# Weight sums of seven-product groups made in device memory instead of on VectorE, and more such groups: eight in each of three down stages, six in each of two

## What is computed

```python
# first block: ffn_w1 is 2048 x 8192, ffn_w2 is 8192 x 2048
hn = rms_norm(h, norm_ffn[i])
h = h + jnp.square(jax.nn.relu(hn @ ffn_w1[i])) @ ffn_w2[i]
...
# second block: w_down is 5632 x 2048
return (jax.nn.silu(gate) * val) @ w_down
```

## Time and profile before

| | us |
|---|---|
| median of 3 runs | 2193.94 (2193.53 to 2194.72) |
| profiled execution | 2195.73 |
| its span, first to last instruction | 2193.9 |
| PE busy | 2180.1 (99%) |
| DVE, ACT, POOL busy | 1566.5, 1133.5, 711.8 |
| the DMA queue that loads weights, share of 16 engines | 55.7% |

### The profile page before, as it was taken

One profiled execution on the slowest core, in us unless ns is written; L12 is line 12 of the kernel. 1 busy time (PEld: TensorE's weight loads), 2 busy tenths in 40 slices (PEclk: granted clock), 3 DMA queues, 4 the chain that ended last, 5 costly groups with the idle time before them and its releaser, 6 DMA issues.

```text
span 2193.9 us, 34076 instructions
## 1 busy us (share of the span) xinstructions
PE 2180.1 (99%) x11511; PEld 1862.4 (85%) x11511; DVE 1566.5 (71%) x2187; ACT 1133.5 (52%) x1720; POOL 711.8 (32%) x625
## 2 busy tenths in 40 slices
PE   9999999999999999999999999999999999999998
PEld 7888988888888888888888887788888888888887
DVE  6876767558657757755878667567778777787775
ACT  6445555545445545454556455465455455554553
POOL 3202320361362263153000033005554355533531
PEclk9999999999999999999999999999999999999999
DMA  7665335556556556566565654545555665555664
GB/s 250 231 224 171 116 130 181 174 184 211 191 182 209 192 184 207 202 194 197 177 199 188 225 171 137 192 163 182 189 195 185 202 198 192 188 191 197 200 207 149
DMA packets 118084, 414.35 MB, mean 189 GB/s; under 512 B 12896, under 2 KB 18048, under 8 KB 117472
## 3 DMA queue, kind: packets, MB, share of 16 engines
q1 hardware_dynamic: 111600, 401.37, 55.7%
q10 hardware_dynamic: 6384, 11.70, 1.7%
HBM read 409.29 MB, written 2.15 MB: 188 GB/s over the span
## 4 chain that ended last, share of the span: by engine, by line
PE 93%; DVE 4%; ACT 1%; DMA 1%; POOL 1%; issue 1%; SPq 0%; DVEq 0%; ACTq 0%; POOLq 0%
PE bank L607 33%; PE bank L615 17%; PE bank L941 6%; PE bank L943 6%; PE bank L942 6%; PE bank L664 2%; PE bank L666 2%; PE bank L665 2%; DVE wboth L1307 2%; PE bank L1269 1%; PE bank L1267 1%; PE bank L1268 1%; PE bank L740 1%; PE bank L1202 1%; PE bank L777 1%; PE bank L917 1%
## 5 line engine op out<-in xcount | busy, mean ns | idle before, releaser
L1307 DVE TENSOR_TENSOR wboth<-raw,wboth 128x1024 fp32r<-128x1024 f32 (+1 forms) x756 | 953.8, 1267 | 468.1 <-ACT wboth L2157 459.8
L2157 ACT CAST wboth<-raw 128x1024 fp32r<-128x1024 f32 (+1 forms) x756 | 773.0, 1034 | 469.3 <-PE bank L943 123.3
L607 PE MATMUL bank<-A,wboth 128*128 128x512 f32 x2928 | 705.4, 392 | 0.5 <-DVE wboth L1307 0.3
L607 PEld LDWEIGHTS bank<-A,wboth 128*128 128x128 f32 x2928 | 536.8, 188 | 105.3 <-issue 1.3
L615 PEld LDWEIGHTS bank<-A,wboth 128*128 128x128 f32 x2928 | 376.7, 191 | 14.8
L615 PE MATMUL bank<-A,wboth 128*128 128x256 f32 x2928 | 384.0, 283 | 0.0
L941 PE MATMUL bank<-wboth,H 128*128 128x512 f32 x508 | 197.8, 389 | 1.2 <-DVE wboth L1307 1.2
L943 PE MATMUL bank<-wboth,H 128*128 128x512 f32 x508 | 197.6, 389 | 0.0
L942 PE MATMUL bank<-wboth,H 128*128 128x512 f32 x508 | 197.6, 389 | 0.0
L2661 POOL TENSOR_TENSOR PT<-z,rs 128x256 f32<-128x256 f32 x88 | 92.5, 1052 | 263.4 <-DVE z L1338 261.3
L2661 POOL TENSOR_TENSOR bias<-z,rs 128x256 f32<-128x256 f32 x64 | 104.7, 1635 | 197.9 <-DVE z L1338 109.4
(11 more groups left out here) (387 smaller groups left out, 3160.7 us busy)
## 6 DMA issues: line engine op xcount, KB each, us to landing
raw<-wstream SPq DMA_DIRECT2D x756, 512.0 KB, 3.4
bias<-bias_rows ACTq DMA_DIRECT2D x6, 512.0 KB, 5.4
x<-xrows ACTq DMA_DIRECT2D x1, 2048.0 KB, 9.1
bias<-grows ACTq DMA_DIRECT2D x2, 1024.0 KB, 6.4
out<-x SPq DMA_DIRECT2D x8, 256.0 KB, 2.1
x<-xT SPq DMA_DIRECT2D x7, 256.0 KB, 5.3
pA<-bias_rows ACTq DMA_DIRECT2D x2, 512.0 KB, 6.9
Sm<-grows ACTq DMA_DIRECT2D x1, 1024.0 KB, 6.6
```

The costliest lines, as they stand in the source:

```text
L607: last = nc.tensor.matmul(bank(j)[:, :], whi[:, s, cols(i)], moving(j, k), start=(k == 0), stop=(k == K - 1))
L1307: V.tensor_tensor(wlo[:, s, 0:w], raw[:, s, 0:w], whi[:, s, 0:w].bitcast(F32), ALU.subtract).then_inc(lo_ready, 1)
L2157: C.copy(whi[:, s, 0:w], raw[:, s, 0:w]).then_inc(hi_ready, 1)
```

## The change

Weight sums are no longer made on the engines. SP copies the two weight pieces of each group into a buffer `weight_sums` in device memory; POOL issues three adding transfers for each group (`accum_op=ALU.add`), which make two more pieces of sums there; SP loads these like weights, but into slots of their own (`y` in the first block, `kT` in the second). ACT and DVE split them as they split pieces. A group is then four pieces of the stream: one whole piece, half a piece, and two pieces of sums.

```diff
+FIRST = Pairing(((2, 3, 5, 6), (2, 3, 5, 6)))
+SECOND = Pairing(((2, 4, 6), (2, 4, 6)))
-FIRST = Pairing(((3, 5), (3, 5)), sides=12, mains=17, last_sides=28)
-SECOND = Pairing(((4, 6), (2, 4, 6)), sides=14, mains=16, last_sides=32)
...
+            def load_sum(c, i, g, h):
+                slots = 1 if is_down2(c) else 2
+                free = pairing(c).groups[g - slots] if g >= slots else None
+                if free:
+                    sp.wait_ge(lo_ready, PB[stage_at(c)[1]] + pairing(c).begin[free[0], free[2]] + 2 + h + 1)
+                to, landed, _ = sum_slot(c, g, h)
+                sp.dma_start(to, weight_sums[2 * group_of(c, g) + h]).then_inc(landed, 16)
...
+            def sum_copy(c, g):
+                if c and g == 0:
+                    sp.wait_ge(sums_copied, 16 * group_of(c, 0))
+                x, n = first_weight(c, g), group_of(c, g)
+                sp.dma_start(weight_sums[2 * n:2 * n + 2], wstream[x:x + 2]).then_inc(sums_copied, 16)
+            copies_in = {"kv": 0, "q": 1, "ff0": 2, "gate": DN, "q2": DN + 1}
...
+                        if name in copies_in and (w - count) % 4 == 3 and (w - count) // 4 < len(pairing(copies_in[name]).groups):
+                            sum_copy(copies_in[name], (w - count) // 4)
```

On PE a group reads the sums from `whi` and `wlo`, and its second product waits for the mix of its pair:

```diff
+                    arrive(i, 2 * m + 1)
+                    product(main_bank(c, cp, 0), *hidden(2 * m + 1, early), *weights(i, 0))
+                    pe.wait_ge(*mix_ready.at(mix_count(c, at.mixed.index(m) + 1)))
+                    product(main_bank(c, cp, 2), *mix_of(m, 3), *weights(i, 1)).then_inc(piece_used, 1)
                     arrive(i + 1)
+                    product(side_bank(c, cp, ONE), *hidden(2 * m, early), *weights(i + 1, 0), lone, final).then_inc(piece_used, 1)
+                    arrive(i + 2)
+                    product(side_bank(c, cp, FIVE), *mix_of(m, 1), *weights(i + 2, 0), lone, final)
+                    product(side_bank(c, cp, SEVEN), *mix_of(m, 0), *weights(i + 2, 1), lone, final).then_inc(piece_used, 1)
+                    arrive(i + 3)
+                    product(side_bank(c, cp, SIX), *mix_of(m, 2), *weights(i + 3, 1), lone, final).then_inc(t_used.sem, 1)
+                    product(main_bank(c, cp, 1), *hidden(2 * m + 1, late), *weights(i + 3, 0)).then_inc(piece_used, 1)
```

DVE loses `t_first`, `t_second`, `t_lows`, ACT loses `t_highs`, POOL loses its `t_first`; in all five stages `sides_in` of the second half now comes behind `mains_in`, as it did before in `dn0` and `dn1` alone:

```diff
-                steps_of.update({at.sides: lambda: sides_in(c, 0), at.mains: lambda: mains_in(c, 0, range(4)), at.last_sides: lambda: sides_in(c, 1),
-                                 30: lambda: mains_in(c, 1, range(2)), 31: lambda: mains_in(c, 1, range(2, 4))})
+                steps_of = {at.over[0]: lambda: sides_in(c, 0), at.middle: lambda: mains_in(c, 0, range(4)),
+                            at.count: lambda: sides_in(c, 1),
+                            at.count - 2: lambda: mains_in(c, 1, range(2)), at.count - 1: lambda: mains_in(c, 1, range(2, 4))}
...
             for f in range(4):
-                pe.wait_ge(*banks_taken.at(8 * (FF_CHUNKS - 1)))
-                if f == 2:
-                    pe.wait_ge(z_ready, 4 + UB["proj"])
+                if f < 2:
+                    pe.wait_ge(z_ready, 4 + UB["proj"] - 2 + 2 * f)
+                else:
+                    pe.wait_ge(*banks_taken.at(8 * (FF_CHUNKS - 1)))
```

POOL issues the adding transfers. `sum_first` adds 256 rows (even calls) or 128 rows (odd calls) of 2 KB from the weights, `sum_last` adds 256 rows of 2 KB from the sums themselves:

```diff
+                pool.wait_ge(sums_copied, 16 * group_of(c + 1, 0))
+                if i % 2:
+                    pool.dma_start(weight_sums[2 * n + 1, :, 0:WIDE], wstream[x + 1, :, WIDE:], accum_op=ALU.add).then_inc(sums_half, 16)
+                else:
+                    pool.dma_start(weight_sums[2 * n].rearrange("p (f w) -> p f w", f=2), wstream[x:x + 2, :, WIDE:].rearrange("a p w -> p a w"),
+                                   accum_op=ALU.add).then_inc(sums_half, 16)
...
+                pool.wait_ge(sums_half, 32 * group_of(c + 1, 0))
...
+            def sums_in_attention(c, i):
+                n = len(pairing(c).groups)
+                if 1 <= i < 2 * n + 1:
+                    sum_first(c, i - 1)
+                if 2 * n + 4 <= i < 3 * n + 4:
+                    sum_last(c, i - 2 * n - 4)
+                if ATT_PIECES - 2 * n <= i:
+                    sum_first(c + 1, i - ATT_PIECES + 2 * n)
...
+                        if c == 1 and it * 4 + j < 2 * len(FIRST.groups):
+                            sum_first(2, it * 4 + j)
...
+                for g in range(len(FIRST.groups)) if c == 1 else ():
+                    pool.wait_ge(piece_used, SLOTS + PB[fd] + 2 + 2 * g)
+                    sum_last(2, g)
```

399 lines of the change are left out of this document (200 added, 199 removed).

## The result

The changed kernel takes **2262.09 us** (median of 4 runs, 2259.29 to 2263.86); the kernel before took 2194.32 us beside it (2193.53 to 2194.72). The ratio is 1.0308, 95% interval 1.0290 to 1.0326: 68 us slower, where 6 us faster was forecast.

A forecast was written before the change was run, and what follows sets the result against it. PE was taken as the bound, busy 2180.1 of 2193.9 us. The terms -9.5 - 1.6 + 0.5 + 1.2 + 3.5 = -5.9 us gave 2188.0 us; the range of all was 2183.5 to 2203.

The forecast's parts named there:

- 14 products, -9.5 us: Down stages: 36 groups in place of 22 save PE 14 products of 0.68 us, 9.5 us, the surest term.
- fd0's jam on DVE, -1.6 us: fd0: DVE's sums go, so PE's wait behind DVE is gained, 1.6 us, bounds 0 and 1.6.
- The mixes one pair earlier, +0.5 us, bounds 0 to 2: fd0's first group, now pair 2: PE waits 0.5 us for POOL's first mix_low; nothing in fd1 or fd2.
- The sides behind the mains, +1.2 us, bounds 0 to 2: Second-half sides are read out in the next stage: PE waits 1.2 us once, in proj behind fd2.
- The attentions have room: 12.6 to 17.4 of 18 us; nothing taken: Attentions: loads, copies and first sums fill 12.6 to 17.4 of 18 us of DMA engine time; no loss.
- Rival 3: Slow adding rows hold POOL at step 20 of q, 2205.5 us; slower total from about 0.26 us a row; chance 0.23.
- fd1, +3.5 us: fd1: last sums beside loads for pairs 5 and 6 make a piece 3.5 us late at 0.1 us per adding row.
- double price: Rival 2: an adding row costs twice a plain one, fd1 loses 9.6 us, 2194.1 us, no change; chance 0.22.
- A load has 5 us in hand in plain pieces: Plain pieces: loads land 3.4 us after issue, issued about 8.6 us before ACT needs them; nothing taken.
- All hidden (2184.5): Rival 1: all transfers are hidden, by loads winning or POOL issuing slowly, -9.4 us, 2184.5 us; chance 0.17.
- wrong if fd0 or fd2 are longer than 83 us too: Sign of being wrong: fd0, fd2 above 83 us, 81.6 expected; then loads alone are too many for groups in a row.
- PE waits for POOL in `q` or `q2`: Sign of being wrong, in the attentions: PE waits for POOL in q or q2.

The follow-up runs named there:

- more_groups: Changed kernel with transfers moved to places with room, sides back ahead of mains, raw slots counted separately, pairs 3, 4, 5 in fd0 to fd2: 2189.85 us.
- two_pairs: Changed kernel with the pairs of fd0 to fd2 set back to 3 and 5, all transfer kinds kept: 2218.52 us, ratio 1.0112.
- two_pairs_none: Changed kernel with pairs 3 and 5 in fd0 to fd2 and neither adding transfers nor copies: 2195.57 us, ratio 1.0006.
- mixes_two: no_transfers with the mixes of pairs 2 and 5 alone, used again by pairs 3 and 6: 2218.74 us, ratio 1.0113.
- late_adds: Changed kernel with adding transfers, and dn0's copies, moved to other places, nothing left out: 2237.69 us, ratio 1.0207.
- no_transfers: Changed kernel without adding transfers and copies, plain weight pieces loaded in place of sums: 2226.94 us, ratio 1.0150.
- ring_alone: no_transfers with only the slot rule changed: pieces that go to raw are counted by themselves, so all four slots serve: 2205.77 us, ratio 1.0052.

## Why the prediction was wrong, point by point

- **14 products, -9.5 us.** Right in size: 42 matmuls fewer, and where nothing else was lost (`fd1` and `fd2` of more_groups) a group gave 0.68 us.
- **fd0's jam on DVE, -1.6 us.** Right for pairs 3 and 5: `fd0` went to 84.4 us in two_pairs and two_pairs_none, 1.5 less. In the change as made it came too, but the first group, one pair earlier and beside `mix_low`, made a larger jam in the same place (4.1 us).
- **The mixes one pair earlier, +0.5 us, bounds 0 to 2.** This step failed. I priced when PE would have its mix, and that was nearly right (0.17 us of wait). I did not price what POOL does to the engine beside it when a group needs its splits just then: splits of 2.18 us, and some 4 us lost at each first group. It was the earlier place that cost this (mixes_two with two mixes still lost 3.2 to 3.8 us, more_groups with three mixes and pair 3 first lost nothing); the two more mixes cost 1.1 us in each hidden stage. The earlier trace rows showed it already: 1.77 us for a first sum beside POOL, 0.68 for the next. I booked it as a stall that goes.
- **The sides behind the mains, +1.2 us, bounds 0 to 2.** The mechanism was right for `proj`, which lost 1.9. "Behind the other stages hidden units use the main banks; dn0 shows no wait" was wrong: `ff1` and `ff2` lost 0.85 us each. That `dn0` and `up1` bear it did not carry over. It is no wait for banks: the splits never got back the 3.2 us by which the sides had put them off. Why they did not was not tried.
- **The attentions have room: 12.6 to 17.4 of 18 us; nothing taken.** The sum of engine time was right at its dear end (the DMA engines were busy for 0.93 of `q` and 0.89 of `q2`). The step from it failed: at such a load every other transfer is late, and I had looked at loads and not at ACT's queue. `q` lost 6.8 and `q2` 5.6. Rival 3, "slower", had its place in the attentions, and PE did wait for POOL's takes, but not because POOL stood at step 20: with 0.17 to 0.18 us a row (12.2% of 16 x 2257.5 us over 24768, and `fd1` above) its condition of 0.26 was not met.
- **fd1, +3.5 us (9.6 at double price).** Right in place and in kind, too small: of 28.1 us, late_adds gives 18.6 back (112.4 to 93.8). At the price of 0.17 the working gives 0.6 x 7 + 3.5 = 7.7 us. Two things are missing from it: it stopped counting at pair 6 of the first half, 34 us into the stage, though loads and last sums went on side by side to 738 us, 60 us into it, and it left out the clock, up to 5.4 us.
- **A load has 5 us in hand in plain pieces.** Right there. I let it stand for groups without working it out. This is the largest miss, 21 us in no_transfers, and it needs no adding transfer: `i % 4` leaves two of four slots empty in a group. A load of piece `i` waits for the split of piece `i - 4`, and in a row of groups that is the load but one before it. Only the distance in pieces was looked at, which had not changed.
- **Rivals.** All hidden (2184.5) and double price (2194.1) both took rows of groups to be free. Of the signs of being wrong that I named, "wrong if fd0 or fd2 are longer than 83 us too" came, 91.6 and 92.1, and so did "PE waits for POOL in `q` or `q2`", 3.6 us once in each; the reading given for the first, "the loads alone are too many for groups in a row", is not what ring_alone showed: the same loads fit, with their slots. The range failed because none of its cases had a loss of more than some 2 us outside the transfers.

The sum, from the runs: adding transfers 33.4 us, copies 1.7, slots of `raw` 21.2, the sides 3.7; that is 60.0 of 67.8 + 9.5 = 77.3 us. Of the other 17, PE's timeline of ring_alone puts 12 at the first groups and halves of `fd0` to `fd2` (3.0, 4.6 and 4.6, the first with the gain of 1.5 in it), and 3.4 in the hidden stages over what the sides cost there. Some 2 us are in no place that I can name.
